# Gathering an expert's tokens with the selection as stationary operand, then turning the rows by eight transposes

## The chip, the cores and the metric

The kernel runs on one core of a Trainium2 chip. The metric is the device time of one execution in microseconds (us). One execution was also taken by the hardware profiler; all durations below come from that one.

## What is computed

The reference is one inference step of a two-layer network on 128 context tokens and 256 latent tokens, each a row of 1024 numbers in float32. Layer 1, the last, ends in a mixture of experts, which is the part that matters here:

```python
logits = (t @ w_router) + b_router              # 384 tokens, 8 experts
top_v, top_i = lax.top_k(logits, TOP_K)         # two experts per token
comb = sum(one_hot(top_i) * softmax(top_v))     # weight of each expert for each token
for e in range(N_EXPERTS):
    y = y + comb[:, e:e + 1] * swiglu(t, w_gate[e], w_up[e], w_down[e])
# swiglu(h) = (silu(h @ w_gate) * (h @ w_up)) @ w_down, 1024 -> 1408 -> 1024
```

## The kernel before, in words

The experts are not run on all tokens. A **job** is one expert with up to 128 of its tokens; an expert with more than 128 tokens gets a second job. The number of jobs is found at run time (`njobs`); in the profiled execution it is nine. TensorE, ScalarE and VectorE each have a loop over the jobs, and order comes from semaphores alone: every engine works through its own list, written out in the program.

Products are made in three terms. Each operand is split into a rounded part (type float32r) and the rest (value minus rounded part, again float32r), and TensorE multiplies rounded by rounded, rest by rounded and rounded by rest (`e_piece`, L1063). An expert's weights come as 36 **pieces** numbered n = 0 to 35: 0 to 7, 8 to 15 and 16 to 23 are gate and up weights of three chunks of columns (512, 512 and 384), 24 to 35 are the down weights (the last two half as large). The path of a piece: SyncE's queue starts the transfer into one of 18 buffers `e_raw` (L536); ScalarE copies it, rounded, into one of four buffers `e_w` (L1541, `e_round`); VectorE subtracts to get the rest (L186, `e_rest`); TensorE multiplies (L578) six times with 512 columns moving (three times for pieces 34 and 35), and counts up `e_used`, which frees the `e_w` buffer. So piece n can be rounded only when TensorE has done with piece n - 4. Here the pieces 36, 37, 38, 39 mean pieces 0 to 3 of the next job.

The **gather** takes a job's tokens out of the 384. `sel` (128 x 128, three of them for the three groups of 128 tokens) holds a one where token t goes to slot s. Before, `gather(part)` (L1078) makes the turned result at once: for each of eight blocks of 128 features the token matrix `hT_parts[part]` is the stationary operand and `sel` the moving one, three matmuls of 128 columns each summed over the token groups, so 24 for a part. Part 0 is the rounded part of the tokens and is gathered after piece 29 (`GATHER_AT`), part 1 the rest, after piece 32. As `sel` is zeros and ones, the gathered parts need no new split: ScalarE copies four banks of PSUM to `hG[0]` and `hG[1]` (L1548). The gather made in job i serves job i + 1; one more stands ahead of the loop. The last job's gather serves nobody.

After piece 35 ScalarE copies the job's result (L1583, two copies `ey`), VectorE makes its rest (L2120, `output_rest`), and TensorE adds it back to the tokens' rows in the next job, by six scatter steps of two matmuls (`scatter`, L1095), each followed by an addition on VectorE (L2113).

Three more steps of a job use TensorE's transposes (L575): eleven for the product of gate and up, in groups of four, four and three, and three for `sel`.

Of the kernel before, what the change touches and what calls it, by code (L numbers as in the profile page):

```python
# [7 lines left out]
P = 128  # L8
DM, DEPTH = 1024, 2
# [3 lines left out]
KD = DM // P  # L13
# [13 lines left out]
NE, DE, KE = 8, 1408, 11  # L27
CHUNKS = ((0, 512), (512, 512), (1024, 384))
DOWN = ((0, 4), (4, 4), (8, 3))
GATHER_AT = (29, 32)  # L30
SCATTER_AT = (3, 5, 7, 9, 11, 13)


# [155 lines left out]
def build(nc, dram, outs, marks):  # L189
# [4 lines left out]
    with ExitStack() as ctx:  # L194
# [107 lines left out]
        hT_parts = parts("htoken", DM, 3, o, o + 3 * DM); o += 6 * DM  # L302
        hG = parts("hG", P, KD, o, o + DM); o += 2 * DM
        eprod = cut("eprod", o, DE); o += DE
        ey = [p_[:, 0, :] for p_ in parts("ey", DM, 1, o, o + DM)]; o += 2 * DM
        eprodT = parts("eprodT", P, KE, o, o + DE); o += 2 * DE
        sel, selT = parts("sel", P, 3, o, o + 3 * P); o += 6 * P
# [245 lines left out]
        def _(pe):  # L553
# [521 lines left out]
                        last = mm(out, x[0][:, k0 + k, :], wl[:, cols_], False, stop)  # L1075
                last.then_inc(s("e_used"), 1)

            def gather(part):  # L1078

                for k in range(KD):  # L1080
                    b = psum[2 - 2 * part + k // 4]
                    for j in range(3):
                        last = mm(b[:, (k % 4) * P:(k % 4 + 1) * P], hT_parts[part][:, j, k * P:(k + 1) * P], sel[:, j, :], j == 0, j == 2)
                    if k % 4 == 3:
                        last.then_inc(s("e_gather"), 1)

            def slots(i):

# [14 lines left out]
                mm(psum[6 + half][:, :], selT[:, j, :], ey[0][:, cols_], True, False)  # L1103
                mm(psum[6 + half][:, :], selT[:, j, :], ey[1][:, cols_], False, True).then_inc(s("e_sc"), 1)

            for k in range(6):
                pe.wait_ge(*at("htok_rounded", k))
            pe.wait_ge(s("e_sel"), 1)
            gather(0)
            for k in range(6):  # L1110
                pe.wait_ge(*drained("htok", k))
            gather(1)
            pe.wait_ge(*at("jobs_ready"))
            njobs = pe.value_load(rt_i[0:1, 0:1], min_val=NE, max_val=NJOB)
            with pe.Fori(0, njobs) as i:

                pe.wait_ge(s("e_hG"), i * 4 + 4)
                for c in range(3):

                    pe.wait_ge(s("e_prod"), i * 3 + 3 + (1 if c == 2 else 0))  # L1120
                    if c == 2:
                        slots(i)
                    for n in range(c * CHUNK_PIECES, (c + 1) * CHUNK_PIECES):
                        which = int(E_PIECES[n][0] == "moe_w_up")
                        e_piece(i, n, hG, lambda k, c0: (psum[2 * (c % 2) + which], k == 0, k == KD - 1))
                        if n in SCATTER_AT:
                            scatter(i, SCATTER_AT.index(n))
                    if c == 1:
                        pe.wait_ge(s("e_sc_done"), i * 6 + 6)
                    if c > 0:  # L1130
                        e_transposes(pe, s, transpose, psum, eprod, i, c - 1)
                for n in range(3 * CHUNK_PIECES, NPC):
                    k0 = E_PIECES[n][1]
                    if k0 == 0:
                        pe.wait_ge(s("e_selT"), i * 2 + 2)
                    if k0 == DOWN[1][0]:
                        e_transposes(pe, s, transpose, psum, eprod, i, 2)
                    for c in range(3):
                        if k0 == DOWN[c][0]:
                            pe.wait_ge(s("e_pT_rest"), i * 3 + c + 1)  # L1140
                    e_piece(i, n, eprodT, lambda k, c0: (psum[4 + (E_PIECES[n][3] + c0) // 512], k == 0, k == KE - 1))
                    if n == GATHER_AT[0]:
                        pe.wait_ge(s("e_sel"), i + 2)
                        gather(0)
                    elif n == GATHER_AT[1]:
                        gather(1)
            pe.wait_ge(s("e_hG"), njobs * 4 + 4)
            for t in range(2):
                for half in range(2):
                    for k in range(4):  # L1150
# [10 lines left out]
        def _(act):  # L1161
# [380 lines left out]

            e_round(0, 0, E_AHEAD)

            def e_gathered(i, part):
                for h in range(2):
                    act.wait_ge(s("e_gather"), i * 4 + 2 * part + h + 1)
                    a(hG[part][:, 4 * h:4 * h + 4, :], psum[2 - 2 * part + h][:, :].rearrange("p (k s) -> p k s", k=4), ACT.Copy)\  # L1548
                        .then_inc(s("e_hG"), 1)

            e_gathered(0, 0)
            e_gathered(0, 1)
            act.wait_ge(*at("jobs_ready"))
            njobs = act.value_load(rt_i[0:1, 0:1], min_val=NE, max_val=NJOB)
            with act.Fori(0, njobs) as i:
                def e_turn(c):
                    act.wait_ge(s("e_pT_full"), i * 3 + c + 1)
                    src, dst, _ = e_turned(psum, eprodT, c)
                    a(dst, src, ACT.Copy).then_inc(s("e_pT"), 1)

                done = E_AHEAD
                for c, (c0, n) in enumerate(CHUNKS):
                    e_round(i, done, CHUNK_PIECES * (c + 1) + E_PARTS - 1)
                    done = CHUNK_PIECES * (c + 1) + E_PARTS - 1
                    act.wait_ge(s("e_used"), i * NPC + E_PARTS + CHUNK_PIECES * (c + 1))
                    act.wait_ge(s("e_prod"), i * 3 + 3 + c)
                    a(esig[:, 0:n], psum[2 * (c % 2)][:, 0:n], ACT.Sigmoid).then_inc(s("e_sig"), 1)
                    if c == 1:
                        act.wait_ge(s("e_selT_full"), i + 1)
                        a(selT, psum[4][:, 0:3 * P].rearrange("p (j s) -> p j s", j=3), ACT.Copy).then_inc(s("e_selT"), 1)  # L1570
                        a(wslot, psum[5][:, 0:1], ACT.Copy).then_inc(s("e_selT"), 1)
                    if c > 0:
                        e_turn(c - 1)
                e_round(i, done, done + 4)
                e_turn(2)
                e_round(i, done + 4, GATHER_AT[0] + E_PARTS)
                e_gathered(i + 1, 0)
                e_round(i, GATHER_AT[0] + E_PARTS, GATHER_AT[1] + E_PARTS)
                e_gathered(i + 1, 1)
                e_round(i, GATHER_AT[1] + E_PARTS, NPC + E_AHEAD)  # L1580
                act.wait_ge(s("e_used"), i * NPC + E_PARTS + NPC)
                for half in range(2):
                    a(ey[0][:, half * 512:(half + 1) * 512], psum[4 + half][:, :], ACT.Copy, scale=wslot).then_inc(s("e_eyr"), 1)  # L1583
# [16 lines left out]
        def _(dve):  # L1600
# [507 lines left out]
            def add_output(i, n_):  # L2108
# [3 lines left out]
                dst = yacc[:, j, half * 512:(half + 1) * 512]  # L2112
                tt(dst, dst, psum[6 + half][:, :], A).then_inc(s("e_sc_done"), 1)  # L2113

            def output_rest(i):

                for half in range(2):
                    dve.wait_ge(s("e_eyr"), i * 2 + half + 1)
                    cols_ = slice(half * 512, (half + 1) * 512)
                    stt(ey[1][:, cols_], psum[4 + half][:, :], wslot, ey[0][:, cols_].bitcast(F32), M, SUB).then_inc(s("e_ey"), 1)  # L2120

            def e_rests(i, n0, n1):
                for n in range(n0, n1):
                    e_rest(dve, s, e_raw, e_w, i, n)

            e_rests(0, 0, E_AHEAD)
            with dve.Fori(0, njobs) as i:

# [23 lines left out]
                        select(lambda at_: bass.ds(code + at_, 1)).then_inc(s("e_sel"), 1)  # L2152
                e_rests(i, done, done + 4)
                e_turn_rest(2)
                e_rests(i, done + 4, NPC + E_AHEAD)
            output_rest(njobs)
            dve.wait_ge(*at("gate_rows"))
            dve.wait_ge(*at("fin_row_in"))
# [106 lines left out]
```

## Time and profile before

| | us |
|---|---|
| median of three runs | 1977.55 |
| lowest and highest | 1976.17, 1981.03 |
| the profiled execution | 1987.14 |
| its span, first to last instruction | 1985.3 |

The loop over the jobs runs from 1440.2 us to about 1962 us of the span. A job takes 57.7 us: the copy of the first gathered bank starts at 1488.67, 1546.38, 1604.15 and 1661.89 us in successive jobs. "PE" is TensorE's matmul stream, "PEld" its loads of stationary operands, "DVE" is VectorE, "ACT" ScalarE, "SPq" SyncE's queue. A row of a timeline gives the start in us from the span's start, the length of the group in us, and the number of instructions; in square brackets stands how long the engine was idle before and what ended the wait. Engines start the next instruction slightly before the record of the one before ends, so the distance between starts is shorter than the recorded duration.

### The profile page before, as it was taken

Reading aid. Unit: us, or ns where it says so; the run is one execution under the profiler, and the core shown is the slowest. Engines: PE = TensorE matmul, PEld = TensorE weight load, DVE = VectorE, ACT = ScalarE, POOL = GpSimd, SP = SyncE. Lnnn points to the kernel's source line nnn. Section 1 sums busy time; section 2 is a strip of 40 time slices with the busy share of each in tenths; the row PEclk is TensorE's granted clock in tenths of the full one; section 3 lists DMA queues with packets and bytes.
Section 4 is the critical chain, followed back from the end, with each engine's and each line's share of the span. In section 5 each row is a group of like instructions: output and inputs, shape, how many; then the busy total and the mean of one; then the engine's idle time right before and its main releaser. Section 6 shows DMA issues by size and latency. Waiting matters only on the chain.

```text
span 1985.3 us, 41063 instructions
## 1 busy us (share of the span) xinstructions
PE 1824.0 (92%) x16663; PEld 1644.4 (83%) x16663; DVE 1101.7 (55%) x1617; ACT 884.8 (45%) x1322; POOL 506.3 (26%) x385
## 2 busy tenths in 40 slices
PE   4998879899999999989979889999799999999996
PEld 3996868787899999989877887879588888888885
DVE  0465678543231111035657875332488888889887
ACT  2445242232343333343532314323367677767765
POOL 0570000243356666656300004425000000000000
PEclk7999989999999999989989899999699999999998
DMA  9347232232434444424542002322678888898880
GB/s 305 110 126 226 68 107 74 84 106 91 132 87 126 126 127 146 139 70 131 173 156 77 5 4 81 116 92 86 220 262 288 299 294 304 300 323 294 287 279 32
DMA packets 225173, 315.30 MB, mean 159 GB/s; under 512 B 15615, under 2 KB 169605, under 8 KB 224901
## 3 DMA queue, kind: packets, MB, share of 16 engines
q1 hardware_dynamic: 217856, 306.22, 47.6%
q10 hardware_dynamic: 7172, 6.97, 1.3%
q8 instruction: 114, 1.87, 0.4%
q14 instruction: 31, 0.25, 0.0%
HBM read 311.05 MB, written 2.10 MB: 158 GB/s over the span
## 4 chain that ended last, share of the span: by engine, by line
PE 77%; DVE 12%; issue 4%; ACT 3%; DMA 2%; ACTq 1%; DVEq 0%; POOL 0%; SPq 0%
PE bank L578 75%; DVE e_w_rest L186 2%; PE bank L575 2%; DMA ring<-in_w_ada 2%; DVE S L1843 1%; ACT e_w_rounded L1541 1%; DVE hT L1625 1%; DVE hT L1619 1%; DVE cvT L1746 1%; DVE ey_rest L2120 1%; ACTq L1172 1%; DMA rows<-in_gn_b 0%; DVE U L1873 0%; DVE St L1895 0%; DVE yT L1967 0%
## 5 line engine op out<-in xcount | busy, mean ns | idle before, releaser
L2197 POOL TENSOR_TENSOR weights_rest<-ring,weights_rounded 128x512 fp32r<-128x512 f32 x344 | 464.0, 1351 | 531.8 <-ACT weights_rounded L1256 530.8
L186 DVE TENSOR_TENSOR e_w_rest<-e_raw,e_w_rounded 128x1024 fp32r<-128x1024 f32 (+1 forms) x327 | 354.3, 1132 | 76.6 <-ACT e_w_rounded L1541 74.3
L1256 ACT ACTIVATE weights_rounded<-ring 128x512 fp32r<-128x512 f32 x344 | 215.7, 630 | 368.8 <-PE bank L578 359.8
L1541 ACT ACTIVATE e_w_rounded<-e_raw 128x1024 fp32r<-128x1024 f32 (+1 forms) x327 | 314.0, 989 | 81.3 <-PE bank L578 79.4
L578 PE MATMUL bank<-h_rounded,weights_rounded 128*128 128x384 f32 x688 | 231.2, 336 | 5.0 <-DVE h_rest L1655 2.7
L578 PE MATMUL bank<-h_rounded,weights_rest 128*128 128x384 f32 x688 | 229.9, 334 | 0.0
L578 PE MATMUL bank<-h_rest,weights_rounded 128*128 128x384 f32 x688 | 229.9, 334 | 0.0
L578 PE MATMUL bank<-e_w_rounded,hG_rounded 128*128 128x512 f32 (+1 forms) x432 | 165.2, 382 | 3.9 <-DVE e_w_rest L186 2.5
L578 PE MATMUL bank<-e_w_rest,hG_rounded 128*128 128x512 f32 (+1 forms) x432 | 162.6, 376 | 0.0
L578 PE MATMUL bank<-e_w_rounded,hG_rest 128*128 128x512 f32 (+1 forms) x432 | 162.0, 375 | 0.0
L578 PE MATMUL bank<-hg_rounded,weights_rounded 128*128 128x384 f32 x384 | 144.1, 375 | 9.3 <-DVE yT L1980 4.8
L578 PEld LDWEIGHTS bank<-h_rounded,weights_rounded 128*128 128x128 f32 x688 | 129.1, 188 | 7.9 <-DVE h_rest L1655 3.9
L578 PE MATMUL bank<-hg_rest,weights_rounded 128*128 128x384 f32 x384 | 130.1, 339 | 0.0
L578 PE MATMUL bank<-hg_rounded,weights_rest 128*128 128x384 f32 x384 | 130.1, 339 | 0.0
L578 PEld LDWEIGHTS bank<-h_rest,weights_rounded 128*128 128x128 f32 x688 | 129.2, 188 | 0.0
L578 PEld LDWEIGHTS bank<-h_rounded,weights_rest 128*128 128x128 f32 x688 | 129.2, 188 | 0.0
L578 PEld LDWEIGHTS bank<-e_w_rounded,hG_rounded 128*128 128x128 f32 x432 | 81.8, 189 | 24.0 <-DVE e_w_rest L186 11.7
L1921 DVE TENSOR_TENSOR tmp<-tmp,bank 128x384 f32<-128x384 f32 x32 | 17.7, 555 | 146.4 <-PE bank L578 146.4
L1640 DVE SCALAR_TENSOR_TENSOR xT<-bank,mods,xT 128x128 f32<-128x128 f32 (+1 forms) x48 | 17.2, 412 | 139.4 <-PE bank L578 139.4
L578 PEld LDWEIGHTS bank<-e_w_rest,hG_rounded 128*128 128x128 f32 x432 | 81.7, 189 | 12.5
L578 PEld LDWEIGHTS bank<-e_w_rounded,hG_rest 128*128 128x128 f32 x432 | 81.8, 189 | 11.6
L578 PEld LDWEIGHTS bank<-hg_rounded,weights_rounded 128*128 128x128 f32 x384 | 73.8, 192 | 18.1 <-issue 10.5
(325 smaller groups left out, 3528.9 us busy)
## 6 DMA issues: line engine op xcount, KB each, us to landing
ring<-in_w_ada SPq DMA_DIRECT2D x96, 512.0 KB, 6.0
e_raw<-in_moe_w_down SPq DMA_DIRECT2D x90, 512.0 KB, 4.6
ring<-in_w_in SPq DMA_DIRECT2D x88, 512.0 KB, 4.7
e_raw<-in_moe_w_gate SPq DMA_DIRECT2D x72, 512.0 KB, 5.8
e_raw<-in_moe_w_up SPq DMA_DIRECT2D x72, 512.0 KB, 7.0
e_raw<-in_moe_w_gate SPq DMA_DIRECT2D x36, 384.0 KB, 4.1
e_raw<-in_moe_w_up SPq DMA_DIRECT2D x36, 384.0 KB, 4.0
ring<-in_ffn_w_gate SPq DMA_DIRECT2D x22, 512.0 KB, 4.9
```

The costliest lines, as they stand in the source:

```text
L186: eng.tensor_tensor(wl, e_raw[n % E_RAW][:, 0:kn * w], wr.bitcast(F32), ALU.subtract).then_inc(s("e_rest"), 1)
L575: return pe.transpose(out, src, ident[0:n, 0:n])
L578: return pe.matmul(out, lhsT, rhs, start=start, stop=stop)
L1172: act.dma_start(rows[r:r + n, g, :], flat(src).rearrange("(r c) -> r c", c=P))\
L1256: a(w_parts[n % NSLOT][0], raw, ACT.Copy).then_inc(*E.up("rounded_ready", *key))
L1541: a(e_w[n % E_PARTS][0][:, 0:kn * w], e_raw[n % E_RAW][:, 0:kn * w], ACT.Copy).then_inc(s("e_rounded"), 1)
L1619: tt(hT[:, 2 * g:2 * g + 2, :], xT[:, 2 * g:2 * g + 2, :], row.rearrange("p (a t) -> p a t", a=1).broadcast_to([P, 2, T]), M)\
L1625: ins = ts(hT[:, k, t0:t1], hT[:, k, t0:t1], modAs[:, l, which, k, s_:s_ + 1], mods[:, l, 24 * which + k, s_:s_ + 1], M, A)
L1746: ins = stt(dst, src, w, dst, M, A)
L1843: tt(S1[:, cp, h0:h0 + 3:2, :], src, msk, M).then_inc(*E.read("pair", l, d, cp, hp))
L2120: stt(ey[1][:, cols_], psum[4 + half][:, :], wslot, ey[0][:, cols_].bitcast(F32), M, SUB).then_inc(s("e_ey"), 1)
L2197: pool.tensor_tensor(wl, raw, wr.bitcast(F32), ALU.subtract).then_inc(*E.up("rest_ready", *key))
```

## The change

The gather's operands swap places. `sel` becomes the stationary operand and the tokens' rows move, 512 columns at a time: for each half of the features six matmuls (two parts by three token groups) sum into one bank. What comes out is a row for each slot, whole, not in parts, and not turned. ScalarE copies it to a new tile `hgt`, which lies in the place of `eprod`. Two pieces later `turn_gathered` turns it with eight transposes into banks 0 and 1, ScalarE rounds these into `hG[0]`, and VectorE, which had no part in it before, subtracts to get `hG[1]` (`hG_rest`). The whole gather now stands after piece 29 and the turning after piece 31. Ahead of the loop the order is gather, turning, rounding, rest, and VectorE does `hG_rest(0)` ahead of the rests of the first three pieces.

```diff
-GATHER_AT = (29, 32)
+GATHER_AT, GATHERED_AT = 29, 31
...
+        hgt = cut("hgt", used["eprod"][0], DM)
...
-            def gather(part):
-
-                for k in range(KD):
-                    b = psum[2 - 2 * part + k // 4]
-                    for j in range(3):
-                        last = mm(b[:, (k % 4) * P:(k % 4 + 1) * P], hT_parts[part][:, j, k * P:(k + 1) * P], sel[:, j, :], j == 0, j == 2)
-                    if k % 4 == 3:
-                        last.then_inc(s("e_gather"), 1)
+            def gather():
+
+                for h in range(2):
+                    n_ = 0
+                    for part in range(2):
+                        for j in range(3):
+                            last = mm(psum[2 + h][:, :], sel[:, j, :], hT_parts[part][:, j, h * 512:(h + 1) * 512], n_ == 0, n_ == 5)
+                            n_ += 1
+                    last.then_inc(s("e_gather"), 1)
+
+            def turn_gathered(i):
+
+                for h in range(2):
+                    pe.wait_ge(s("e_hgt"), i * 2 + h + 1)
+                    for k in range(4):
+                        last = transpose(psum[h][:, k * P:(k + 1) * P], hgt[:, (4 * h + k) * P:(4 * h + k + 1) * P])
+                    last.then_inc(s("e_hT_full"), 1)
...
-            for k in range(6):
-                pe.wait_ge(*at("htok_rounded", k))
             pe.wait_ge(s("e_sel"), 1)
-            gather(0)
             for k in range(6):
                 pe.wait_ge(*drained("htok", k))
-            gather(1)
+            gather()
+            turn_gathered(0)
...
-                pe.wait_ge(s("e_hG"), i * 4 + 4)
+                pe.wait_ge(s("e_hG"), i * 2 + 2)
...
-                    if n == GATHER_AT[0]:
+                    if n == GATHER_AT:
                         pe.wait_ge(s("e_sel"), i + 2)
-                        gather(0)
-                    elif n == GATHER_AT[1]:
-                        gather(1)
-            pe.wait_ge(s("e_hG"), njobs * 4 + 4)
+                        gather()
+                    elif n == GATHERED_AT:
+                        turn_gathered(i + 1)
+            pe.wait_ge(s("e_hG"), njobs * 2 + 2)
...
-            def e_gathered(i, part):
+            def e_gathered(i):
+
                 for h in range(2):
-                    act.wait_ge(s("e_gather"), i * 4 + 2 * part + h + 1)
-                    a(hG[part][:, 4 * h:4 * h + 4, :], psum[2 - 2 * part + h][:, :].rearrange("p (k s) -> p k s", k=4), ACT.Copy)\
-                        .then_inc(s("e_hG"), 1)
-
-            e_gathered(0, 0)
-            e_gathered(0, 1)
+                    act.wait_ge(s("e_gather"), i * 2 + h + 1)
+                    a(hgt[:, h * 512:(h + 1) * 512], psum[2 + h][:, :], ACT.Copy).then_inc(s("e_hgt"), 1)
+
+            def e_hG_round(i):
+
+                for h in range(2):
+                    act.wait_ge(s("e_hT_full"), i * 2 + h + 1)
+                    a(hG[0][:, 4 * h:4 * h + 4, :], psum[h][:, :].rearrange("p (k s) -> p k s", k=4), ACT.Copy)\
+                        .then_inc(s("e_hG_rounded"), 1)
+
+            e_gathered(0)
+            e_hG_round(0)
...
-                e_round(i, done + 4, GATHER_AT[0] + E_PARTS)
-                e_gathered(i + 1, 0)
-                e_round(i, GATHER_AT[0] + E_PARTS, GATHER_AT[1] + E_PARTS)
-                e_gathered(i + 1, 1)
-                e_round(i, GATHER_AT[1] + E_PARTS, NPC + E_AHEAD)
+                e_round(i, done + 4, GATHER_AT + E_PARTS)
+                e_gathered(i + 1)
+                e_round(i, GATHER_AT + E_PARTS, GATHERED_AT + E_PARTS)
+                e_hG_round(i + 1)
+                e_round(i, GATHERED_AT + E_PARTS, NPC + E_AHEAD)
...
+            def hG_rest(i):
+
+                for h in range(2):
+                    dve.wait_ge(s("e_hG_rounded"), i * 2 + h + 1)
+                    tt(hG[1][:, 4 * h:4 * h + 4, :], psum[h][:, :].rearrange("p (k s) -> p k s", k=4),
+                       hG[0][:, 4 * h:4 * h + 4, :].bitcast(F32), SUB).then_inc(s("e_hG"), 1)
+
...
+            hG_rest(0)
             e_rests(0, 0, E_AHEAD)
...
-                e_rests(i, done + 4, NPC + E_AHEAD)
+                e_rests(i, done + 4, GATHERED_AT + E_PARTS)
+                hG_rest(i + 1)
+                e_rests(i, GATHERED_AT + E_PARTS, NPC + E_AHEAD)
```

## Rows read from the trace of the kernel before

**Rows 1.** The page, first part: span; busy us, share and instructions of each engine.

```profile
span 1985.3 us, 41063 instructions
...
PE 1824.0 (92%) x16663; PEld 1644.4 (83%) x16663; DVE 1101.7 (55%) x1617; ACT 884.8 (45%) x1322; POOL 506.3 (26%) x385
```

**Rows 2.** The page's chain of waits: share of the span by engine.

```profile
PE 77%; DVE 12%; issue 4%; ACT 3%; DMA 2%; ACTq 1%; DVEq 0%; POOL 0%; SPq 0%
```

**Rows 3.** Windows (columns: length, each engine's busy us, granted clock, DMA share, GB/s).

```profile
1426.00:1440.20 14.20, 13.36 (x64) 13.17 (x62) 7.93 (x29) 4.79 (x7) 0.20 (x1) 0.50 0.34 102
...
1504.40:1562.10 57.70, 56.86 (x290) 48.18 (x290) 49.36 (x60) 40.94 (x51) 0.00 (x0) 1.00 0.88 300
...
1908.50:1966.00 57.50, 56.76 (x308) 49.22 (x308) 48.36 (x60) 39.63 (x49) 0.00 (x0) 1.00 0.38 127
```

**Rows 4.** Waits in seven jobs, 1504.4 to 1908.5: waited in total, times, longest.

```profile
DVE e_w_rest L186 <- ACT e_w_rounded L1541: 51.0, 21, 4.2
...
PEld bank L578 <- DVE e_w_rest L186: 16.9, 28, 1.0
```

**Rows 5.** Groups of instructions from 1200 us on: count, busy us, mean ns.

```profile
L578 PE MATMUL bank<-ey_rounded,sel_rest 128*128 128x512 f32 x60 | 24.5, 409 | 2.7 <-DVE yacc L2113 2.6
...
L575 PE MATMUL bank<-first,eprod 128*128 128x128 f32 x99 | 15.2, 272 | 0.0
```

**Rows 6.** Timeline of TensorE's weight loads: start, us, count, idle before, releaser.

```profile
1482.59 0.19 PEld L578 LDWEIGHTS bank<-e_w_rounded,eprodT_rounded 128*128 128x128 f32 x1 [0.97 <-DVE e_w_rest L186]
...
1483.86 0.48 PEld L575 LDWEIGHTS bank<-first,eprod 128*128 128x128 f32 x3
...
1484.42 0.19 PEld L578 LDWEIGHTS bank<-e_w_rounded,eprodT_rest 128*128 128x128 f32 x1
...
1486.95 2.88 PEld L578 LDWEIGHTS bank<-sel_rounded,htoken_rounded 128*128 128x128 f32 x24
...
1493.77 2.87 PEld L578 LDWEIGHTS bank<-sel_rounded,htoken_rest 128*128 128x128 f32 x24
...
1499.68 0.19 PEld L578 LDWEIGHTS bank<-e_w_rounded,hG_rounded 128*128 128x128 f32 x1 [0.51 <-DVE e_w_rest L186]
...
1504.40 0.19 PEld L578 LDWEIGHTS bank<-e_w_rounded,hG_rounded 128*128 128x128 f32 x1 [0.75 <-DVE e_w_rest L186]
...
1525.05 0.59 PEld L575 LDWEIGHTS bank<-first,eprod 128*128 128x128 f32 x4
```

**Rows 7.** Timeline of ScalarE over the same handover.

```profile
1488.67 0.60 ACT L1548 ACTIVATE hG_rounded<-bank 128x512 fp32r<-128x512 f32 x1 [1.60 <-PE bank L578]
...
1497.32 2.96 ACT L1541 ACTIVATE e_w_rounded<-e_raw 128x1024 fp32r<-128x1024 f32 x3
1500.17 1.25 ACT L1583 ACTIVATE ey_rounded<-bank,wslot 128x512 fp32r<-128x512 f32 x2
```

**Rows 8.** Timeline of VectorE over the same handover.

```profile
1498.40 3.50 DVE L186 TENSOR_TENSOR e_w_rest<-e_raw,e_w_rounded 128x1024 fp32r<-128x1024 f32 x3 [4.22 <-ACT e_w_rounded L1541]
1501.81 1.40 DVE L2120 SCALAR_TENSOR_TENSOR ey_rest<-bank,wslot,ey_rounded 128x512 fp32r<-128x512 f32 x2
1503.13 3.49 DVE L186 TENSOR_TENSOR e_w_rest<-e_raw,e_w_rounded 128x1024 fp32r<-128x1024 f32 x3
```

**Rows 9.** Timeline of weight loads: two of the scatter.

```profile
1505.66 0.19 PEld L578 LDWEIGHTS bank<-ey_rounded,sel_rest 128*128 128x128 f32 x1
...
1505.89 0.19 PEld L578 LDWEIGHTS bank<-ey_rest,sel_rest 128*128 128x128 f32 x1
```

**Rows 10.** Timelines before the first job: TensorE's weight loads, then VectorE.

```profile
1428.81 5.24 PEld L578 LDWEIGHTS bank<-sel_rounded,htoken_rounded 128*128 128x128 f32 x24
...
1440.22 0.29 PEld L578 LDWEIGHTS bank<-e_w_rounded,hG_rounded 128*128 128x128 f32 x1 [1.05 <-issue]
...
1430.66 3.50 DVE L186 TENSOR_TENSOR e_w_rest<-e_raw,e_w_rounded 128x1024 fp32r<-128x1024 f32 x3 [1.24 <-issue]
```

**Rows 11.** Timeline of VectorE after the last job.

```profile
1963.74 1.40 DVE L2120 SCALAR_TENSOR_TENSOR ey_rest<-bank,wslot,ey_rounded 128x512 fp32r<-128x512 f32 x2
```

## The prediction

> **What bounds the kernel now.** I read the page's busy shares first: TensorE is busy 92% of the span and no other engine over 55% [rows 1]. The chain of waits says the same, 77% of it on TensorE and 12% on VectorE [rows 2]. An average hides the stage, so next I took windows over the stage that the change touches, the job loop. Its window of one job shows TensorE busy 56.86 of 57.70 us, VectorE 49.36, ScalarE 40.94, the clock granted in full, the DMA engines at a share of 0.88 with 300 GB/s [rows 3]. So TensorE's work sets the job, but VectorE is close behind. The waits show where it already cuts in: in seven jobs TensorE's loads waited 16.9 us for `e_w_rest`, 2.4 us a job, while VectorE waited 51.0 us for ScalarE's roundings, 7.3 us a job [rows 4]. The timelines place both. TensorE stands at 1482.59 (0.97 us), 1499.68 (0.51) and 1504.40 (0.75) [rows 6]. VectorE stands just before, at 1498.40 for 4.22 us [rows 8]: the second half of the gather, from 1493.77 on [rows 6], feeds no piece, frees no buffer and holds ScalarE at its wait for it, so ScalarE rounds pieces 36 to 38 only from 1497.32 [rows 7]. Then VectorE works without a gap through three rests, two `output_rest` and the rest of piece 39 [rows 8], and that is what TensorE waits for twice. The gather costs its own time and these two stalls.
>
> **Prices.** All distances are between starts. A gather matmul of 128 columns with its load takes at most (2.88 - 0.19) / 23 = 0.117 us [rows 6], so 48 take 5.6. A matmul with 512 columns takes 0.23 (1505.66 to 1505.89, the scatter [rows 9]); that is the nearest row for the new gather, though one is recorded as 409 ns [rows 5], as records overlap. The new gather: 12 x 0.23 = 2.76. A transpose: three of them put the next piece's second load 0.56 after the first transpose's load, where 0.23 is usual, so 0.33 for three, 0.11 each; a group of four lasts 0.59, so 0.15 each [rows 6]. I take 0.125, eight are 1.0. From outside, 0.11 and the full record of 272 ns [rows 5] bound it: 0.9 and 2.2 for eight. TensorE's own work falls by 5.6 - 3.76 = 1.8 us a job at most. The lag from a bank's last matmul to ScalarE's start: by distances the first bank's 12 matmuls end at 1486.95 + 12 x 0.117 = 1488.35, the copy starts at 1488.67 [rows 6, 7]: 0.32. ScalarE: three roundings of 1024 columns at 0.95, the last 1.06 long; a bank's copy 0.60; the two `ey` copies 1.25 [rows 7]. VectorE: a rest (3.50 - 1.22) / 2 = 1.14 with 1.22 recorded, two 128x512 operations 1.32 from start to start of the next, so 0.7 each [rows 8].
>
> **The handover between two jobs, anew.** Time zero is the end of piece 29 on TensorE, 1486.95 [rows 6]; before, piece 39 starts at 17.45 (1504.40).
>
> TensorE: gather banks at 1.38 and 2.76; piece 30 to 4.14, piece 31 to 5.52; transposes to 6.02 and 6.52; piece 32 to 7.90, 33 to 9.28, 34 to 9.97, 35 to 10.66.
>
> ScalarE: copies to `hgt` 1.70 to 2.30 and 3.08 to 3.68, long before 5.52, so the new wait on `e_hgt` holds nobody. Queued behind the second copy is the rounding of piece 33, free to start since piece 29's end: 3.6 to 4.66, its rest by 5.9, wanted at 7.90. Piece 34 (half size, 0.63 as an estimate from the 1.06) 4.55 to 5.2. `e_hG_round` 6.34 to 6.94 and 6.9 to 7.5. Behind it piece 35: 7.5 to 8.1. Then 36, held by piece 32's end plus lag: 8.22 to 9.28; 37: 9.60 to 10.66; 38: 10.55 to 11.6; `ey` 11.5 to 12.75; 39: 12.65 to 13.7.
>
> VectorE: the two new `hG_rest` 6.96 to 7.64 and 7.6 to 8.3 at 0.7 each; the rest of 35 by 9.0; 36 9.30 to 10.52 (wanted at 10.66); 37 from 10.68; 38 from 11.82; `output_rest` from 12.96; 39 from 14.28 to 15.50.
>
> So `hG` is ready at 8.3 and wanted at 10.66, a margin of 2.4; the stall of 0.51 goes, since ScalarE no longer stands through the gather just before the handover. Piece 39 could start on TensorE at 10.66 + 3 x 1.38 = 14.8, but its rest is late, as before: it starts at 15.55, a stall of 0.75 in place of 0.75. The gain is 17.45 - 15.55 = 1.9 us. From there the queues stand to each other as before (TensorE starts piece 39 when VectorE has just finished its rest), so the later stall of 0.97 stays. VectorE's two new operations, 1.4 us a job, lie in its 7.3 us of waiting for ScalarE [rows 4]; without that cover they would cost their 1.4. ScalarE has four copies as before. SyncE's queue sees its buffers freed earlier: a job in 55.8 us wants 310 GB/s; 300 at a share of 0.88 [rows 3] makes room for 340, so transfers stay hidden.
>
> Nine jobs make eight handovers: 15.2 us. In the last job the same chain leads to `output_rest` at 1963.74 [rows 11], which now starts 1.9 earlier. Together 17.1.
>
> **Ahead of the loop** the clock is at half, 0.50 [rows 3]: a part of the gather takes 5.24 [rows 10]. At doubled prices the gather runs from 1428.81 to 1434.3 and the transposes to 1436.3; ScalarE is through 0.3 + 0.6 later, 1437.2, VectorE's second `hG_rest` at 1437.9. Now the order counts: the rests of the first three pieces, at 1430.66 before [rows 10], stand behind it. The first is ready at 1439.1, and TensorE starts then in place of 1440.22 [rows 10]. Gain 1.1. What the clock does I can't work out: it is granted at half throughout 1426 to 1440.2 though TensorE is busy 13.36 of 14.20 us. If the 8 us of new work pulled its rise forward by half of it, 2 us more are saved; the other way 2 are lost.
>
> **The sum:** 15.2 + 1.9 + 1.1 = 18.2 us. The profiled execution would go from 1987.14 (span 1985.3) to 1969. It lies 9.6 us over the median of the three runs, 1977.55, which I take as the base: 1977.55 - 18.2 = 1959.3.
>
> **Rivals.**
> A, the transposes don't overlap and cost their whole record, 0.272, and with them the turn holds the chain longer: everything after it comes 1.2 later, piece 39 at 16.75, gain 0.7 a job and nothing ahead of the loop, 6.3 in all: 1971. For it: the record is that long [rows 5]. Against: the eleven of a job show 0.11 to 0.15 [rows 6]. The Trainium skill, "TensorE: Matmul & The Clock Gate", Part 4 (PE-mode transpose), gives about 275 ns for one in a kernel; the trace's record of 272 agrees, its distances don't, and by the page's figure this case would hold.
> B, the stall before piece 39 closes too, for instance because VectorE's queue runs a little faster than I add up: 0.75 x 8 = 6 more, 1953.
> C, VectorE binds: with 50.8 us of work in 55.8 the rests of 36 to 39 come later than worked out (36 has 0.14 us to spare) by about 1.4, the size of the added work. Gain 0.5 a job, 5.6 in all: 1972.
> D, slower: TensorE's clock falls after the turn. Place: eight transposes in a row among pieces 30 to 35, where now no group is longer than four. Price: at half clock a piece takes 1.38 more, so from two pieces a job at half clock on the gain is gone (2.8 against 1.9); with three it is 4.1 - 1.9 = 2.2 a job, some 20 in all: 1997. Against: the clock is 1.00 in the windows of jobs that hold fourteen transposes [rows 3]. The skill's same section says that transposes don't count as activity for the clock; the rows show no trace of that, but eight in a row and a stall beside them stand nowhere in them.
>
> **Chances.** Forecast 0.70 (1956 to 1964), A 0.08, B 0.08, C 0.10, D 0.04. About 0.3% (6 us) is what a measurement of this kernel tells from no change. Faster: the forecast, B, and a little over half of A and C: 0.88; the rest of these same, 0.08; slower 0.04. The range, 1953 to 1971, takes in B and nearly all of A, and half of C.
>
> **What would show it.** `hG_rest` on VectorE ends before piece 33 does; the gather takes 2.8 us and the eight transposes 0.9 to 1.2; a job takes 55.8 us instead of 57.7; the wait of 0.51 before piece 36 is gone and one of about 0.75 before piece 39 remains; the loop starts about 1 us earlier. Wrong would be: a wait of TensorE on `hgt` or `hG`, a clock below 1.00 in the loop, transposes 0.27 apart, or ScalarE waiting for a transfer.

## The result

The changed kernel takes 1961.24 us in the median of six runs (1952.28 to 1967.45), the kernel before 1980.62 in six (1976.17 to 1986.12). The ratio is 0.9908, with a 95% interval of 0.9885 to 0.9931; of 1980.62 that is 18.2 us (13.7 to 22.8), while the two medians lie 19.4 apart. Forecast were 18.2, from the base of three runs. Single executions of either kernel lie up to 15 us apart, so the account is kept in the traces' stages. The page after, against [rows 1]; its chain of waits has the shares of [rows 2] to the percent:

```profile
span 1950.5 us, 40528 instructions
...
PE 1788.8 (92%) x16383; PEld 1606.8 (82%) x16383; DVE 1113.3 (57%) x1637; ACT 883.3 (45%) x1322; POOL 505.4 (26%) x385
```

The span is 34.8 us shorter than before, but not all of that is the change. The first gather matmul's load starts at 1415.47 us instead of 1428.81, and nothing ahead of it was changed: I take these 13.3 us as the difference of two executions, for in the profiles of the experiments the same load starts anywhere from 1415.6 to 1428.5 us with the new form, and at 1424.2 and 1427.9 with the old. From that load to the end it is 535.0 us instead of 556.5, and these 21.5 us are the change's in this pair of traces. They come from four places: 3.4 ahead of the loop (8.03 us from the gather to the first piece, 11.41 before), 0.7 in the first job up to its gather, 15.4 in eight handovers, 2.0 after the last.

A job's window (same columns as [rows 3]) is 55.8 us long:

```profile
1486.80:1542.60 55.80, 54.78 (x264) 45.82 (x263) 50.67 (x62) 40.96 (x51) 0.00 (x0) 1.00 0.92 310
```

VectorE's busy time went from 49.36 to 50.67 us, by its two new subtractions; TensorE's from 56.86 to 54.78; the DMA share from 0.88 to 0.92 at 310 GB/s, and ScalarE never waits for a transfer. The waits over seven jobs, against [rows 4]:

```profile
DVE e_w_rest L186 <- ACT e_w_rounded L1549: 25.6, 21, 3.0
...
PEld bank L579 <- DVE e_w_rest L186: 15.6, 28, 1.0
```

VectorE's waiting for ScalarE fell from 51.0 to 25.6 us: half of the cover in which the new work was put is used up or gone. TensorE's waiting for VectorE is 15.6 us, 2.2 a job, hardly less than the 2.4 before.

The handover on TensorE's weight loads, against [rows 6]. The gather runs from 1469.49 (its first three loads) and is over at 1472.24, the turn starts at 1475.00:

```profile
1469.49 0.65 PEld L579 LDWEIGHTS bank<-htoken_rounded,sel_rounded 128*128 128x128 f32 x3
...
1472.24 0.19 PEld L579 LDWEIGHTS bank<-e_w_rounded,eprodT_rounded 128*128 128x128 f32 x1
...
1475.00 1.03 PEld L576 LDWEIGHTS bank<-first,hgt 128*128 128x128 f32 x8
...
1480.14 0.19 PEld L579 LDWEIGHTS bank<-e_w_rounded,hG_rounded 128*128 128x128 f32 x1 [0.17 <-DVE e_w_rest L186]
...
1485.02 0.19 PEld L579 LDWEIGHTS bank<-e_w_rounded,hG_rounded 128*128 128x128 f32 x1 [0.88 <-DVE e_w_rest L186]
```

ScalarE, against [rows 7], copies the two gathered banks and, after two pieces, rounds the two turned ones:

```profile
1471.30 0.60 ACT L1557 ACTIVATE hgt<-bank 128x512 f32<-128x512 f32 x1 [1.70 <-PE bank L579]
1472.66 0.60 ACT L1557 ACTIVATE hgt<-bank 128x512 f32<-128x512 f32 x1 [0.76 <-PE bank L579]
...
1475.86 1.09 ACT L1563 ACTIVATE hG_rounded<-bank 128x512 fp32r<-128x512 f32 x2 [1.14 <-PE bank L576]
```

VectorE, against [rows 8]:

```profile
1474.24 1.83 DVE L186 TENSOR_TENSOR e_w_rest<-e_raw,e_w_rounded 128x1024 fp32r<-128x1024 f32 x2 [3.02 <-ACT e_w_rounded L1549]
1476.49 1.29 DVE L2134 TENSOR_TENSOR hG_rest<-bank,hG_rounded 128x512 fp32r<-128x512 f32 x2 [0.43 <-ACT hG_rounded L1563]
...
1478.86 3.66 DVE L186 TENSOR_TENSOR e_w_rest<-e_raw,e_w_rounded 128x1024 fp32r<-128x1024 f32 x3 [0.48 <-ACT e_w_rounded L1549]
1482.43 1.40 DVE L2142 SCALAR_TENSOR_TENSOR ey_rest<-bank,wslot,ey_rounded 128x512 fp32r<-128x512 f32 x2
1483.75 3.49 DVE L186 TENSOR_TENSOR e_w_rest<-e_raw,e_w_rounded 128x1024 fp32r<-128x1024 f32 x3
```

Set against the handover worked out, with 1469.49 as time zero: first copy 1.81 (forecast 1.70), turn 5.51 (5.52), rounding 6.37 (6.34), `hG_rest` 7.00 to 8.29 (6.96 to 8.3), rest of piece 36 at 9.37 (9.30), `output_rest` 12.94 (12.96), rest of 39 at 14.26 (14.28), piece 39 on TensorE 15.53 (15.55).

### The profile page after: what moved, and what is told of

Its sections match the earlier page's. It is cut to its first block, busy times and chain, and to the rows that moved or that the text cites. A ratio compares the mean times of both kernels' runs of the same rounds, so it can differ in the third digit from the quotient of the medians.

```text
span 1950.5 us, 40528 instructions
## 1 busy us (share of the span) xinstructions
PE 1788.8 (92%) x16383; PEld 1606.8 (82%) x16383; DVE 1113.3 (57%) x1637; ACT 883.3 (45%) x1322; POOL 505.4 (26%) x385
## 4 chain that ended last, share of the span: by engine, by line
PE 77%; DVE 12%; issue 4%; ACT 3%; DMA 2%; ACTq 1%; DVEq 0%; POOL 0%; SPq 0%
PE bank L579 75%; PE bank L576 2%; DVE e_w_rest L186 2%; DMA ring<-in_w_ada 2%; DVE S L1858 1%; ACT e_w_rounded L1549 1%; DVE cvT L1761 1%; DVE hT L1640 1%; DVE hT L1634 1%; DVE U L1888 1%; DMA xin<-in_x_sample 0%; DVE yT L1982 0%; DVE St L1910 0%; DVE tmp L1776 0%; DVE hg_rest L1670 0%
## 5 line engine op out<-in xcount | busy, mean ns | idle before, releaser
L579 PEld LDWEIGHTS bank<-hg_rounded,weights_rounded 128*128 128x128 f32 x384 | 73.2, 191 | 18.2 <-issue 10.7
```

The costliest lines, as they stand in the source:

```text
L579: return pe.matmul(out, lhsT, rhs, start=start, stop=stop)
```

## Experiments

The theory on trial, **1**: the gain of a job is what TensorE saves by sending 512 columns per loaded weight instead of 128, less the transposes, and it passes whole through the chain of freed buffers to piece 39. Its rivals: the gain is one of order (ScalarE no longer held just before the handover); VectorE, at 50.7 of 55.8 us, sets the job. Lengths of a job below are distances between the first gathered bank's copy in successive jobs; they repeat within about 0.1 us inside a trace, where a whole execution moves by 15. So where a variant was executed only once, its jobs are compared and not its time. The fences below are timelines as in [rows 6 to 8]: start, us, engine, line, operation, count, and in brackets the wait before.

### The old form at the new places

```diff
-GATHER_AT = (29, 32)
+GATHER_AT = (29, 31)
```

> The kernel before with its second half of the gather moved from after piece 32 to after piece 31: the old form (48 matmuls of 128 columns) at the new places. Theory 1 (the gain of 1.92 us a job is mostly TensorE's own work, 5.4 us of gather against 2.8 + 1.0): TensorE does as much as before; only the 0.51 us stall before piece 36 goes, and VectorE's chain of rests 37, 38, output_rest, 39 then starts at 12.3 after the end of piece 29, so piece 39 starts at 17.2 in place of 17.45: a job takes 57.45 us (57.7 before, 55.8 after). Theory 2 (what counted was that ScalarE is not held at the gather just before the handover; the form is worth little): a job takes under 56.6 us, half of the gain or more.

Measured: ratio 0.9979 (0.9953 to 1.0006). ScalarE's timeline gives the job, 1487.61 to 1545.12, 57.51 us:

```profile
1487.61 0.60 ACT L1548 ACTIVATE hG_rounded<-bank 128x512 fp32r<-128x512 f32 x1 [1.60 <-PE bank L578]
...
1545.12 0.60 ACT L1548 ACTIVATE hG_rounded<-bank 128x512 fp32r<-128x512 f32 x1 [1.60 <-PE bank L578]
```

Its weight loads, the gather's first half and the two waits:

```profile
1485.89 2.88 PEld L578 LDWEIGHTS bank<-sel_rounded,htoken_rounded 128*128 128x128 f32 x24
...
1498.28 0.19 PEld L578 LDWEIGHTS bank<-e_w_rounded,hG_rounded 128*128 128x128 f32 x1 [0.17 <-DVE e_w_rest L186]
...
1503.16 0.19 PEld L578 LDWEIGHTS bank<-e_w_rounded,hG_rounded 128*128 128x128 f32 x1 [0.91 <-DVE e_w_rest L186]
```

The wait before piece 36 fell from 0.51 to 0.17, that before 39 rose from 0.75 to 0.91: order alone is worth 0.2 us of the 1.9. The form is worth the rest, 57.51 - 55.82 = 1.7. The ratio alone could not have told: its interval takes in 1, no change.

### Every transpose twice

```diff
-                    for k in range(4):
+                    for k in (0, 1, 2, 3, 0, 1, 2, 3):
                         last = transpose(psum[h][:, k * P:(k + 1) * P], hgt[:, (4 * h + k) * P:(4 * h + k + 1) * P])
```

> The changed kernel with each of the eight transposes of a turn issued twice into the same place (16 in all). Theory 1 (a transpose costs its distance of about 0.125 us, and TensorE's later start of piece 32 passes through the freed buffers to the whole chain up to piece 39): the second eight take 1.0 us and a job 56.8 us in place of 55.8. Rival (they cost their whole record of 0.27 each): 58.0 us a job. Rival (hidden behind VectorE's chain, since piece 39 waits 0.9 us for its rest anyway): under 0.3 us, a job of 55.8 to 56.1.

Measured in one execution: a job 56.70 us (1477.26 to 1533.96), 0.88 more than 55.82. The sixteen are one row of the weight loads:

```profile
1480.96 1.90 PEld L576 LDWEIGHTS bank<-first,hgt 128*128 128x128 f32 x16
...
1491.86 0.19 PEld L579 LDWEIGHTS bank<-e_w_rounded,hG_rounded 128*128 128x128 f32 x1 [0.85 <-DVE e_w_rest L186]
```

Sixteen last 1.90 us where eight lasted 1.03, so eight more cost 0.87 in the row and 0.88 in the job, 0.11 each, the lower of the two distances that [rows 6] gave and not the record of 272 ns [rows 5]. TensorE still waits 0.85 us before piece 39: the added time is not absorbed there, it shifts both sides of the wait.

### VectorE's two subtractions twice

```diff
+                    tt((spare if h == 0 else esig).rearrange("p (k s) -> p k s", k=4), psum[h][:, :].rearrange("p (k s) -> p k s", k=4),
+                       hG[0][:, 4 * h:4 * h + 4, :].bitcast(F32), SUB)
                     tt(hG[1][:, 4 * h:4 * h + 4, :], psum[h][:, :].rearrange("p (k s) -> p k s", k=4),
                        hG[0][:, 4 * h:4 * h + 4, :].bitcast(F32), SUB).then_inc(s("e_hG"), 1)
```

> The changed kernel with VectorE's two subtractions of hG_rest done twice (the extra ones into spare tiles): 1.3 us more of VectorE's work a job, put where it waits. Theory 1 (the cover is VectorE's wait for ScalarE: hG_rest ends 8.3 us after piece 29's end and the rest of piece 36 can start at 9.4, with the rest of 35 of 0.6 between): the extra 1.3 us fills the free 0.5 + 0.4 first, then delays the chain by about 0.8: a job takes 56.6 us in place of 55.8. Rival (all of VectorE's work is on the path, since it is busy 50.7 of 55.8): 57.1. Rival (free): 55.8.

Measured in one execution: a job 56.27 us, 0.45 more. Its VectorE and its weight loads:

```profile
1477.56 0.69 DVE L2135 TENSOR_TENSOR spare<-bank,hG_rounded 128x512 f32<-128x512 f32 x1 [0.43 <-ACT hG_rounded L1564]
...
1479.96 4.09 DVE L186 TENSOR_TENSOR e_w_rest<-e_raw,e_w_rounded 128x512 fp32r<-128x512 f32 x4
```

```profile
1480.70 0.19 PEld L580 LDWEIGHTS bank<-e_w_rounded,eprodT_rounded 128*128 128x128 f32 x1 [0.35 <-DVE e_w_rest L186]
...
1481.83 0.19 PEld L580 LDWEIGHTS bank<-e_w_rounded,hG_rounded 128*128 128x128 f32 x1 [0.60 <-DVE e_w_rest L186]
...
1486.55 0.19 PEld L580 LDWEIGHTS bank<-e_w_rounded,hG_rounded 128*128 128x128 f32 x1 [0.75 <-DVE e_w_rest L186]
```

The order of things is as expected, the size half of it. The four subtractions take 2.4 us from the first start to the start of what follows (1477.56 to 1479.96), two took 1.2. Of the 1.2 us more, 0.48 filled the wait that stood before the rest of 36 (it is gone from VectorE's rows), some 0.2 were won back because the roundings of 36 to 38 now lie ready, and 0.45 came through, as TensorE's waits of 0.35, 0.60 and 0.75. Neither rival (0 or 1.3) holds: VectorE had cover for some 0.7 us more, not for 1.2.

### Rests before hG_rest(0), ahead of the loop

```diff
-            hG_rest(0)
             e_rests(0, 0, E_AHEAD)
+            hG_rest(0)
```

> The changed kernel with VectorE's rests of the first three pieces put back ahead of hG_rest(0). Before the loop TensorE waits 2.6 us for e_w_rest in the changed kernel. Theory 1 (that wait is VectorE's order: the first rest starts only when hG_rest is done): piece 0 starts as soon as hG_rest is done, 1.1 us earlier, some 6.9 us after the gather's first load in place of 8.0 where the clock rises at the same place; a job still takes 55.8 us. Rival (the handover chain of ScalarE and the semaphores sets it): no change. Also read off: the clock before the loop. [...]

Measured in one execution: a job 55.80 us; from the gather's first load to the first piece's 8.38 us, not 6.9. Missed. TensorE's weight loads:

```profile
1421.43 0.54 PEld L579 LDWEIGHTS bank<-htoken_rounded,sel_rounded 128*128 128x128 f32 x3
...
1429.81 0.29 PEld L579 LDWEIGHTS bank<-e_w_rounded,hG_rounded 128*128 128x128 f32 x1 [4.23 <-issue]
```

Its VectorE, from the end of the job list on:

```profile
1423.47 0.17 DVE L2115 CAST rt<-rt 128x17 int32<-128x17 f32 x1
1424.89 3.50 DVE L186 TENSOR_TENSOR e_w_rest<-e_raw,e_w_rounded 128x1024 fp32r<-128x1024 f32 x3 [1.25 <-issue]
1428.30 1.28 DVE L2134 TENSOR_TENSOR hG_rest<-bank,hG_rounded 128x512 fp32r<-128x512 f32 x2
```

In this execution the clock was up before the gather began, so `hG` could be rounded from 1425.01 on. VectorE was not ready: it makes the job list until 1423.6 and starts the rests at 1424.89, in whichever order, and with all three first the subtractions end at 1429.6. Where the gather starts at half clock, VectorE could start a rest 3.4 us before the first turned bank is rounded (1417.3 and 1420.77 in the changed kernel), and the order would help. I had taken that case for the only one. It also cost something behind: during TensorE's wait of 4.2 us the clock fell to 1.2 GHz, and it stayed there until 1435.3, through the first two pieces.

### The fourth piece before the job's result

```diff
-E_AHEAD = E_PARTS - 1
+E_AHEAD = E_PARTS
...
-                        e_rests(i, done, SCATTER_AT[n_] + E_AHEAD)
-                        done = SCATTER_AT[n_] + E_AHEAD
+                        e_rests(i, done, SCATTER_AT[n_] + E_PARTS - 1)
+                        done = SCATTER_AT[n_] + E_PARTS - 1
```

> The changed kernel with E_AHEAD = 4 in place of 3: ScalarE rounds and VectorE subtracts piece 39 (piece 3 of the next job) before the copies of the job's result and output_rest, not behind them. Theory 1 (what TensorE still waits for before piece 39, 0.9 us, is the place of piece 39 behind output_rest on VectorE; but VectorE has only some 0.5 us of waits from there up to piece 27, so most of what is won comes back as waiting there): the wait before 39 is gone, those up to piece 27 grow from 1.16 to about 1.5, and a job takes 55.3 us in place of 55.8. Rival (it is a local wait and nothing comes back): 54.9. Rival (the later output_rest makes TensorE's first scatter wait as long): 55.8.

Measured: ratio 0.9865 (0.9833 to 0.9896), a job 55.09 us (1480.62 to 1535.71), 0.73 less. TensorE's weight loads after its waits:

```profile
1529.54 0.19 PEld L579 LDWEIGHTS bank<-e_w_rounded,eprodT_rounded 128*128 128x128 f32 x1 [0.97 <-DVE e_w_rest L186]
...
1550.58 0.19 PEld L579 LDWEIGHTS bank<-e_w_rounded,hG_rounded 128*128 128x128 f32 x1 [0.23 <-DVE e_w_rest L186]
```

The job lies between the 55.3 of my theory and the 54.9 of its rival. The wait before 39 is gone, a small one of 0.23 stands a piece later, and the one before piece 27 is 0.97 as ever. Nothing came back there: the claim that VectorE works at its limit from the handover to piece 27 is wrong. What does come back comes once, behind the last job: `output_rest` there starts one rest later (12.3 us after the first gathered bank's copy, 11.1 before), and the kernel ends 33.8 us after that copy in place of 32.7. The edit also puts a fourth piece's rounding and rest ahead of the loop.

### The select behind two rests

```diff
-                    if c == 2:
-                        dve.wait_ge(s("e_selT_full"), i + 1)
-                        code = dve.value_load(rt_i[0:1, bass.ds(i + 19, 1)], min_val=0, max_val=NCODE - 1)
-                        select(lambda at_: bass.ds(code + at_, 1)).then_inc(s("e_sel"), 1)
-                e_rests(i, done, done + 4)
+                e_rests(i, done, done + 2)
+                dve.wait_ge(s("e_selT_full"), i + 1)
+                code = dve.value_load(rt_i[0:1, bass.ds(i + 19, 1)], min_val=0, max_val=NCODE - 1)
+                select(lambda at_: bass.ds(code + at_, 1)).then_inc(s("e_sel"), 1)
+                e_rests(i, done + 2, done + 4)
```

> The changed kernel with VectorE's select (six operations, 0.9 us with their register load, for the next job's gather) moved behind the rests of pieces 27 and 28. Theory 1 (the wait of 0.97 us before piece 27 is VectorE's burst at the end of the third chunk: two products, a turned rest and the select ahead of the rest of piece 27; the pieces behind have room for the select, with the transposes of the product giving TensorE 0.3 us of other work): the wait before 27 falls to 0.1 to 0.2 and a job takes 55.0 us in place of 55.8. Rival (VectorE is saturated, the wait shows up again before piece 29 or 30): 55.8.

Measured: ratio 0.986 (0.9825 to 0.9894), a job 55.04 us. The same view:

```profile
1527.27 0.19 PEld L579 LDWEIGHTS bank<-e_w_rounded,eprodT_rounded 128*128 128x128 f32 x1 [0.19 <-DVE e_w_rest L186]
...
1547.15 0.19 PEld L579 LDWEIGHTS bank<-e_w_rounded,hG_rounded 128*128 128x128 f32 x1 [0.90 <-DVE e_w_rest L186]
```

As forecast: 0.97 became 0.19, nothing appears behind it, and the wait before 39 is untouched.

### All three orders

The two edits above and, ahead of the loop:

```diff
+            e_rests(0, 0, 1)
             hG_rest(0)
-            e_rests(0, 0, E_AHEAD)
+            e_rests(0, 1, E_AHEAD)
```

> The changed kernel with both (fourth piece first, select behind two rests) and, ahead of the loop, VectorE's rest of piece 0 before hG_rest(0) and the other rests behind it. Theory 1 (the two waits are coupled through VectorE's continuous work from output_rest to piece 27): the waits of 0.9 and 0.97 us fall to 0 and 0.5, a job takes 54.5 us, and the whole 11 us less than the changed kernel, a ratio to the kernel before of about 0.985. Rival (they add up): 54.0 and 0.983. Rival (no gain beyond the better one): 55.0 and 0.987. The clock before the loop is read here too: full before the gather ends if the new form raises it.

Measured: 1945.93 us in the median of six runs (1941.44 to 1953.59), ratio 0.9828 (0.9799 to 0.9856); a job 54.31 us (1471.05 to 1525.36). The same view:

```profile
1519.19 0.19 PEld L579 LDWEIGHTS bank<-e_w_rounded,eprodT_rounded 128*128 128x128 f32 x1 [0.20 <-DVE e_w_rest L186]
...
1540.22 0.19 PEld L579 LDWEIGHTS bank<-e_w_rounded,hG_rounded 128*128 128x128 f32 x1 [0.21 <-DVE e_w_rest L186]
```

The window of one of its jobs:

```profile
1486.00:1540.30 54.30, 54.30 (x264) 45.82 (x263) 50.47 (x62) 40.93 (x51) 0.00 (x0) 1.00 0.94 319
```

The two gains add up to the hundredth, 55.82 - 0.73 - 0.78 = 54.31, again against the coupling that I had expected, though nearer to 54.5 than to the rival's round 54.0. The records of TensorE's matmuls now fill the window, 54.30 of 54.30 us; on its loads four waits of 0.2 a job are left. Ahead of the loop, gather to first piece takes 7.05 us: one rest before `hG_rest(0)` saves the 1.0 that three did not:

```profile
1425.63 0.19 PEld L579 LDWEIGHTS bank<-e_w_rounded,hG_rounded 128*128 128x128 f32 x1 [1.82 <-issue]
```

After this wait of 1.8 us the clock stayed at 2.4 GHz. This version beats both kernels: its ratio's interval lies below that of the changed kernel (0.9885 to 0.9931).

### The old form with two orders

The kernel before, with the edits of "The fourth piece before the job's result" and "The select behind two rests".

> The kernel before (old gather, 48 matmuls, two halves) with the same two moves: fourth piece first and select behind two rests. Theory 1: the waits of 0.75 us before piece 39 and 0.97 before piece 27 shrink to about 0 and 0.5; the 0.5 before piece 36 stays, since it is ScalarE standing at the gather's second half; a job takes 56.5 us in place of 57.7, and the distance to the changed kernel with the same moves stays at 1.9 to 2.0. Rival (the new form's gain is the same slack by another way): the distance shrinks to under 1.3 us a job. Ahead of the loop the old form should again run at half clock up to piece 0, if the form and not chance sets it.

Measured: ratio 0.9907 (0.9875 to 0.9939); jobs of 56.43 and 56.33 us. ScalarE's first copy in two jobs, then TensorE's loads after its waits:

```profile
1482.99 0.60 ACT L1548 ACTIVATE hG_rounded<-bank 128x512 fp32r<-128x512 f32 x1 [1.61 <-PE bank L578]
...
1539.42 0.60 ACT L1548 ACTIVATE hG_rounded<-bank 128x512 fp32r<-128x512 f32 x1 [1.60 <-PE bank L578]
```

```profile
1533.34 0.19 PEld L578 LDWEIGHTS bank<-e_w_rounded,eprodT_rounded 128*128 128x128 f32 x1 [0.19 <-DVE e_w_rest L186]
...
1550.43 0.19 PEld L578 LDWEIGHTS bank<-e_w_rounded,hG_rounded 128*128 128x128 f32 x1 [0.48 <-DVE e_w_rest L186]
```

The waits are 0.19 before piece 27, 0.48 before 36 as expected, and none before 39 (no wait stands between 36 and a load 17 us later). With the same orders the new form is 2.05 us a job ahead (56.4 to 54.3). Taking the shared waits away did not shrink its gain: it is not slack won in another way.

### The same rows in narrow matmuls

```diff
-                    n_ = 0
-                    for part in range(2):
-                        for j in range(3):
-                            last = mm(psum[2 + h][:, :], sel[:, j, :], hT_parts[part][:, j, h * 512:(h + 1) * 512], n_ == 0, n_ == 5)
-                            n_ += 1
+                    for c in range(4):
+                        n_ = 0
+                        for part in range(2):
+                            for j in range(3):
+                                last = mm(psum[2 + h][:, c * P:(c + 1) * P], sel[:, j, :], hT_parts[part][:, j, h * 512 + c * P:h * 512 + (c + 1) * P], n_ == 0, n_ == 5)
+                                n_ += 1
```

> The changed kernel with each gather matmul of 512 columns cut into four of 128: the selection stays stationary, the rows still move and are turned, but there are 48 matmuls and 48 loads as in the kernel before. Theory 1 (the form wins only because a matmul carries four times the columns for one load; a 128-column one costs 0.112 us, load-bound): the gather takes 5.4 us in place of 2.8, a job 58.4 us, more than the 57.7 of the kernel before, as the transposes come on top. Rival (the stationary selection itself is cheaper, or the added time is hidden before piece 39's rest): under 57 us. [...]

Measured in one execution: a job 58.43 us, by ScalarE's copies:

```profile
1487.02 0.60 ACT L1558 ACTIVATE hgt<-bank 128x512 f32<-128x512 f32 x1 [2.94 <-PE bank L579]
1489.70 0.60 ACT L1558 ACTIVATE hgt<-bank 128x512 f32<-128x512 f32 x1 [2.08 <-PE bank L579]
...
1545.45 0.60 ACT L1558 ACTIVATE hgt<-bank 128x512 f32<-128x512 f32 x1 [2.94 <-PE bank L579]
```

The second bank comes 2.68 us after the first, where the wide form takes 1.36. This is the other half of the proof: with the selection stationary and the turn kept, but 48 matmuls of 128 columns, the change costs 0.7 us a job instead of winning 1.9. Ahead of the loop it says nothing of what raises the clock, which was already full in this execution when the gather began.

## Why the prediction was right

**What bounds, and the removed stall.** TensorE's work sets the job: right. The 0.51 us wait before piece 36, which I laid on ScalarE standing at the gather's second half, fell to 0.17, not to 0; the old form with that half one piece earlier shows the same 0.17. The cause is shown, its worth is 0.2 of 1.9 us; the other 1.7 are TensorE's own work, 5.4 - 2.75 - 0.9, and the old form at the new places is 1.7 longer.

**The prices.** Twelve matmuls of 512 columns took 2.75 us (1469.49 to 1472.24; 2.76 forecast). Transposes cost 0.11 by doubling, 0.125 was taken, so eight are 0.9 and not 1.0. The removed gather was priced at most 5.6; the narrow variant's banks are 2.68 us apart, so it was 5.4. A semaphore's lag, 0.32, was 0.1 short for the first copy, where nothing waits for it.

**The chain through freed buffers.** Every time of the handover that is set against the rows above held within 0.11 us, and a job's 55.82 us against 55.8. The two directions from which I bounded it were tested: TensorE's work put back passes through whole (0.88 of 0.87), VectorE's only in part (0.45 of 1.2). That the later wait before piece 39 remains (0.88 in this handover, 0.91 in the next) is what lets both be read, since it moves with TensorE's buffers and does not absorb them.

**The rivals.** A (transposes at their whole record) fell with the doubled turn; B (the wait before 39 closes) did not come by itself, it needed another order; C (VectorE binds) did not come either: the rest of piece 36 started 0.07 us later than worked out and not 1.4; the doubled subtractions put VectorE's room at some 0.7 us, so it was near; D (the clock falls behind the eight transposes) is not there: 1.00 in all windows of jobs, and with sixteen transposes too. What the Trainium skill says in "TensorE: Matmul & The Clock Gate", Part 4 (PE-mode transpose), that transposes don't count as activity, stays untested: eight of them last 1.0 us here and the clock stayed up. Its 275 ns for one agrees with the recorded 272 and not with what eight more cost.

**Ahead of the loop** one term was mis-sized: 1.1 us forecast, 3.4 measured, and 0.7 more in the first pieces. The mechanism named for it, rests behind `hG_rest(0)`, is in the rows, TensorE's load waits for `e_w_rest` for 2.78 us:

```profile
1415.47 0.97 PEld L579 LDWEIGHTS bank<-htoken_rounded,sel_rounded 128*128 128x128 f32 x3
1416.54 1.18 PEld L579 LDWEIGHTS bank<-htoken_rest,sel_rounded 128*128 128x128 f32 x3
1417.82 0.67 PEld L579 LDWEIGHTS bank<-htoken_rounded,sel_rounded 128*128 128x128 f32 x3
...
1423.50 0.19 PEld L579 LDWEIGHTS bank<-e_w_rounded,hG_rounded 128*128 128x128 f32 x1 [2.78 <-DVE e_w_rest L186]
```

VectorE in the same stretch:

```profile
1420.77 0.69 DVE L2134 TENSOR_TENSOR hG_rest<-bank,hG_rounded 128x512 fp32r<-128x512 f32 x1 [4.68 <-ACT hG_rounded L1563]
...
1422.23 3.48 DVE L186 TENSOR_TENSOR e_w_rest<-e_raw,e_w_rounded 128x1024 fp32r<-128x1024 f32 x3
```

But I had priced the gather at half clock to its end. By the starts of these groups of three, the first loads come 0.36 and 0.43 us apart, the third group's 0.24: TensorE went from 1.2 to 2.4 GHz 2.3 us into the gather. The windows show it by the granted clock (the third figure from the end):

```profile
1415.47:1417.47 2.00, 2.00 (x7) 1.61 (x7) 0.54 (x5) 0.00 (x0) 0.00 (x0) 0.50 0.11 38
1418.00:1424.50 6.50, 3.70 (x19) 2.73 (x19) 3.57 (x5) 3.34 (x5) 0.00 (x0) 1.00 0.01 2
1424.70:1428.00 3.30, 3.30 (x9) 2.52 (x9) 3.30 (x4) 1.06 (x1) 0.00 (x0) 0.50 0.80 256
```

So the gather took 3.75 us and not 5.5, and from its end to the end of the second `hG_rest` it was 3.1 us and not 3.6: that is the 2.3 missing here. In the first pieces the kernel before stood at half clock for 5.0 us and the changed one for 3.4. I had written that the clock couldn't be worked out and bounded its effect by 2 us either way; the two stretches together gave 3.0 us more than forecast, beyond that bound, and within the range of the whole. No run holds the clock still while the form changes, so this share rests on the rows and not on an experiment.

**The base, and luck.** The forecast was set from the median of three runs, 1977.55, which three more moved to 1980.62. 1959.3 was forecast and 1961.24 measured; from the profiled execution it would have been 1969, since 9.6 us of that one's time are its own. That the gain of 18.2 us was met to the tenth is luck: the measured one is known to 4.6 us either way, and the traces, which carry the job's gain to 0.1 us, put the change at 21.5, as they hold the 3.0 us that the sum lacked ahead of the loop and in the first pieces.

## What to carry to other kernels

A matmul with 128 moving columns and a weight load of its own costs 0.112 us here, one with 512 columns 0.23: four times the columns for twice the time. Where a small matrix (a selection, a mask) meets a large one, make the small one stationary and send the large one in full rows, and turn the result: 12 wide matmuls and 8 transposes beat 48 narrow ones by 1.7 us a job (57.51 against 55.82), though they add a round trip through two other engines. Lay the round trip under work that is already supplied, and then look where the wait that remains stands on the supplying engine: moving six small operations and one piece in its queue won 1.5 us a job, against 1.9 for the whole change.

## What the runs showed of the hardware that was not expected

Ahead of the loop, all three profiles with the narrow old gather (before, and two experiments) stayed at 1.2 GHz for its whole 10.2 us and up to the first piece, 11.4 us in all. In the new form six profiles came to the gather at 1.2 GHz, and in all six the clock rose to 2.4 GHz 2.3 to 2.8 us into it. Two came with the clock already up: with wide matmuls (`e6_rests_first`) and with narrow ones (`e9_narrow_gather`), and both kept it to the gather's end, the narrow ones for 5.4 us. What of the new form brings the rise isn't shown: no execution had the stationary selection, narrow, starting at half clock. After the rise a wait of 2.8 us on TensorE was followed by 1.2 GHz from about 1424.6 to 1428.1 us in the changed kernel, from 1.1 us into the first piece on. With all three orders, where that wait is 1.8 us, no fall followed, and the first job took 45.4 us up to its gathered copy: 47.8 in the changed kernel, 47.8 with the fourth piece's order alone and 47.1 with the select's. The further 1.6 us are near half of the 3.4 us that the others spent at 1.2 GHz there. In the jobs, with waits of at most 1 us, the granted clock stayed at 1.00.

A transpose of 128 x 128 in float32 is recorded as 272 ns and costs 0.11 us in a row of others; in a stream, a record's length is no price.
